# Expert layers of a 512-token block stack: fetch of the first token blocks, split of the first expert's weights and the late rows' bias placed differently

## The reference, cut to what matters

```python
h = rmsnorm(x, ffn_norm[i]) * (1.0 + sc2) + sh2            # adaptive norm
x = x + g2 * hier_moe(h, ...)                              # i = 0, 1

def hier_moe(h, ...):
    g_logits = t @ w_grp + b_grp                           # 4 groups
    g_top, g_idx = top_k(softmax(g_logits), 1)             # one group for a token
    e_logits = (t @ w_rt + b_rt) as (T, 4, 4)
    e_top, e_idx = top_k(e_logits of the group, 2)         # two of its 4 experts
    w = softmax(e_top) * g_top
    hidden = silu(t @ w_gate) * (t @ w_up) * combine       # 16 experts, 1024 -> 256
    return hidden @ w_down                                 # 256 -> 1024
```

## Time and profile before

| | us |
|---|---|
| three timed runs | 3829.78, 3834.50, 3834.51 (median 3834.5) |
| the profiled execution's own time | 3830.91 |
| span of its trace | 3828.5 |
| layer 0: norm, router, experts | from 481.8, 509.5, 542.9 |
| layer 1: norm, router, experts | from 1184.2, 1210.8, 1244.4 |

### The profile page before, as it was taken

One profiled execution on the slowest core, in us unless ns is written; L12 is line 12 of the kernel. 1 busy time (PEld: TensorE's weight loads), 2 busy tenths in 40 slices (PEclk: granted clock), 3 DMA queues, 4 the chain that ended last, 5 costly groups with the idle time before them and its releaser, 6 DMA issues. The chain is left out here.

```text
span 3828.5 us, 45287 instructions
## 1 busy us (share of the span) xinstructions
PE 3060.7 (80%) x15491; PEld 2457.1 (64%) x15491; DVE 2435.3 (64%) x4029; ACT 1271.8 (33%) x2122; POOL 821.3 (21%) x607
## 2 busy tenths in 40 slices
PE   5989849967886899494378464877788999999995
PEld 2876736647665666241256353777788888888884
DVE  1767646545675564566733556887763777877777
ACT  2335334434552543012101012254443333333331
POOL 0001110310120012000012001365453433433331
PEclk9999979988997999696689686898889999999998
DMA  4851359943034896521000012215556888888884
GB/s 181 306 212 31 115 194 359 358 168 118 1 113 158 332 355 252 188 76 36 14 14 1 6 61 67 66 64 164 156 174 237 311 314 333 321 325 327 323 323 176
DMA packets 229526, 701.46 MB, mean 183 GB/s; under 512 B 30054, under 2 KB 109030, under 8 KB 210806
## 3 DMA queue, kind: packets, MB, share of 16 engines
q1 hardware_dynamic: 182428, 478.19, 34.6%
q0 software_dynamic: 46944, 221.27, 15.9%
HBM read 642.20 MB, written 57.18 MB: 183 GB/s over the span
## 5 line engine op out<-in xcount | busy, mean ns | idle before, releaser
L441 PE MATMUL peer_chunks_low<-peer_chunks_down_hi,peer_chunks_bent_hi 128*128 128x512 f32 x768 | 300.1, 391 | 3.6 <-DVE peer_chunks_bent_lo L2751 3.3
L443 PE MATMUL peer_chunks_low<-peer_chunks_down_hi,peer_chunks_bent_lo 128*128 128x512 f32 x768 | 301.0, 392 | 0.0
L442 PE MATMUL peer_chunks_low<-peer_chunks_down_lo,peer_chunks_bent_hi 128*128 128x512 f32 x768 | 300.8, 392 | 0.0
L1350 DVE TENSOR_TENSOR moe_blocks_gu_lo<-moe_raw,moe_blocks_gu_hi 128x2048 fp32r<-128x2048 f32 x112 | 251.6, 2287 | 76.5 <-ACT moe_blocks_gu_hi L1314 76.5
L2625 POOL DMA_INDIRECT peer_chunks_got_up<-in_peer_u_rows,peer_rows_at x128 | 199.9, 1562 | 283.6 <-DVE peer_chunks_got_up L2755 272.7
L441 PE MATMUL peer_chunks_risen<-peer_h_hi,peer_chunks_up_hi 128*128 128x384 f32 x640 | 216.2, 338 | 5.5 <-DVE peer_chunks_up_lo L2732 5.4
L443 PE MATMUL peer_chunks_risen<-peer_h_hi,peer_chunks_up_lo 128*128 128x384 f32 x640 | 215.6, 337 | 0.0
L442 PE MATMUL peer_chunks_risen<-peer_h_lo,peer_chunks_up_hi 128*128 128x384 f32 x640 | 215.1, 336 | 0.0
L1314 ACT CAST moe_blocks_gu_hi<-moe_raw 128x2048 fp32r<-128x2048 f32 x112 | 207.6, 1906 | 15.9 <-DMA moe_raw<-in_moe_gate_up 7.3
L441 PE MATMUL moe_blocks_risen<-moe_blocks_gu_hi,moe_blocks_h_hi 128*128 128x512 f32 x448 | 198.5, 443 | 12.8 <-DVE moe_blocks_gu_lo L1350 8.0
L2631 POOL DMA_INDIRECT peer_chunks_got_down<-in_peer_v,peer_rows_at x128 | 131.3, 1026 | 270.7 <-DVE mod L2767 264.3
(11 more groups left out here) (658 smaller groups left out, 8097.9 us busy)
## 6 DMA issues: line engine op xcount, KB each, us to landing
moe_raw<-in_moe_gate_up SPq DMA_DIRECT2D x32, 2048.0 KB, 9.6
hT<-in_peer_u SPq DMA_DIRECT2D x128, 512.0 KB, 6.9
hT<-in_peer_v SPq DMA_DIRECT2D x128, 512.0 KB, 5.3
fox_o<-in_side_w SPq DMA_DIRECT2D x72, 512.0 KB, 5.9
peer_w<-peer_ahead_stage SPq DMA_DIRECT2D x24, 1024.0 KB, 6.7
peer_chunks_weights<-peer_w SPq DMA_DIRECT2D x128, 192.0 KB, 5.2
moe_raw_dn<-in_moe_down SPq DMA_DIRECT2D x16, 1024.0 KB, 8.9
hT<-in_moe_down SPq DMA_DIRECT2D x16, 1024.0 KB, 7.2
```

The lines of the kernel that those rows point to most:

```text
L441: nc.tensor.matmul(out, l_hi, r_hi, start=start, stop=False)
L442: nc.tensor.matmul(out, l_hi, r_lo, start=False, stop=False)
L443: return nc.tensor.matmul(out, l_lo, r_hi, start=False, stop=stop)
L1350: v.tensor_tensor(gu_lo[:, n % 2, quarter(q)], raw[:, n % GU_SLOTS, quarter(q)], gu_hi[:, n % 2, quarter(q)].bitcast(F32), ALU.subtract).t ...
```

## The change: what it does

- The norm's SP list loads the router's three constants, before the experts' weights, and no longer waits for the stores of `h`; the tiles (`moe_normed`) now live through the router too. The semaphore `rows_out` of the stores goes along to the router.
- The router's POOL list issues the gathers of the first two blocks, after a wait for `rows_out` and for `moe_token`.
- The router's ACT list rounds expert 0's weights before it copies late rows, and its DVE list subtracts at its end (`moe_first_hi`, `moe_first_lo`, which then serve as slot 0 of the pair `gu_hi`, `gu_lo`).
- The experts' stage begins without these, SP's load of step 2 waits for no split, and the first product waits for no split.
- `LateRows`, wherever it stands: POOL's three additions are gone. PE adds the bias by a second matmul of one row into the same bank.

```diff
 class LateRows
     def gpsimd(self, pool):
         self.nc.gpsimd.memset(self.ones[:], 1.0).then_inc(self.filled, 1)
-        pool.wait_ge(self.bias_in, 16)
-        for j in self.ORDER:
-            pool.wait_ge(self.sums_in[j], 16)
-            self.nc.gpsimd.tensor_tensor(self.sums[0:1, j], self.sums[0:1, j], self.bias[:, j], ALU.add).then_inc(self.biased, 1)
     def sum(self, pe, steps):
             pe.wait_ge(self.filled, 1)
-            pe.wait_ge(self.biased, n // self.halves + 1)
+            pe.wait_ge(self.bias_in, 16)
+            pe.wait_ge(self.sums_in[j], 16)
-            self.nc.tensor.matmul(self.banks[n % 2], self.ones[:], self.sums[:, j, columns], start=True, stop=True).then_inc(self.late_summed, 1)
+            self.nc.tensor.matmul(self.banks[n % 2], self.ones[:], self.sums[:, j, columns], start=True, stop=False)
+            self.nc.tensor.matmul(self.banks[n % 2], self.ones[0:1], self.bias[:, j, columns], start=False, stop=True).then_inc(self.late_summed, 1)
 def normed
                         sp.dma_start(rows_dram[t * P:(t + 1) * P], h[:, t]).then_inc(rows_out, 16)
-                    sp.wait_ge(rows_out, 16 * TILES)
 def route
             def _(sp):
-                sp.dma_start(b[:], b_dram).then_inc(loaded, 16)
-                sp.dma_start(earlier[:], earlier_dram).then_inc(loaded, 16)
-                sp.dma_start(number[:], number_dram).then_inc(loaded, 16)
                 late.sync(sp, -1)
             def _(pool):
                 late.gpsimd(pool)
+                pool.wait_ge(rows_out, 16 * TILES)
+                pool.wait_ge(kept, 1)
+                for b in range(2):
+                    pool.indirect_dma_start(rows[:, b], None, rows_dram,
+                                            bass.IndirectOffsetOnAxis(ap=at.token[:, b:b + 1], axis=0)).then_inc(g.rows_in[b], 16)
             def _(act):
                 nc.scalar.activation(ratio[:], gap[:], ACT.Exp).then_inc(raised_ready, 1)
+                act.wait_ge(w_in[0], 16)
+                for part in halves:
+                    nc.scalar.copy(gu_hi[:, part], raw[:, 0, part]).then_inc(gu_rounded, 1)
                 late.keep(act, range(6))
             def _(dve):
                 v.tensor_copy(at.weight[:], table[:, :, 1:]).then_inc(kept, 1)
+                for n, part in enumerate(halves):
+                    dve.wait_ge(gu_rounded, n + 1)
+                    v.tensor_tensor(gu_lo[:, part], raw[:, 0, part], gu_hi[:, part].bitcast(F32), ALU.subtract).then_inc(gu_split, 1)
 def expert_blocks
                 def load_gu(n):
-                    if n >= GU_SLOTS:
-                        sp.wait_ge(gu_split, QUARTERS * (n - GU_SLOTS + 1))
+                    if n > GU_SLOTS:
+                        sp.wait_ge(gu_split, QUARTERS * (n - GU_SLOTS))
-                fetch_rows(0)
-                fetch_rows(1)
-                round_gu(0)
                 round_rows(0)
                 round_gu(1)
-                split_gu(0)
                 split_rows_of(0)
                 split_gu(1)
 def moe
         def early_loads(sp):
+            for dst, src in ((given.b, a["moe_b_route"][layer]), (given.earlier, a["earlier"]), (given.number, a["number"])):
+                sp.dma_start(dst[:], src).then_inc(given.loaded, 16)
             for n in range(GU_SLOTS):
                 sp.dma_start(raw[:, n], gate_up[n]).then_inc(w_in[n], 16)
```

More of the change, by code:

```diff
@@ L315, in scalar, with normed @@
             self.keep(act, range(3 * self.halves))
-def normed(nc, g, name, kind, gain=None, first=None, rows_dram=None, early_loads=None, route_w=None, logits=None):
+def normed(nc, g, name, kind, gain=None, first=None, rows=None, rows_dram=None, rows_out=None, early_loads=None, route_w=None, logits=None):
     SHIFT, SCALE = 0, 1
     with Stage(nc, name) as s:
-        SLOTS = 2 if rows_dram is None else TILES
-        h = s.sb("h", [P, SLOTS, D])
+        SLOTS = 2 if rows is None else TILES
+        h = s.sb("h", [P, SLOTS, D]) if rows is None else rows
         square = s.sb("square", [P, D])
@@ L932, in _, with route @@
                 divide(LOOPS - 1, LOOP - 1)
-def route(nc, g, name, logits, b_dram, earlier_dram, number_dram, at, late):
+def route(nc, g, name, logits, given, early, at, rows, rows_dram, rows_out, raw, gu_hi, gu_lo, w_in, late):
     N, MORE = GROUPS + EXPERTS, TOKEN_BLOCKS - GROUPS
     with Stage(nc, name) as s:
-        b = s.sb("b", [P, N])
-        earlier, number = s.sb("earlier", [P, P]), s.sb("number", [P, TILES])
+        s.adopt([given.loaded, rows_out], early)
+        b, earlier, number, loaded = given.b, given.earlier, given.number, given.loaded
         earlier_ones = s.sb("earlier_ones", [P, 2, P], BF16)
@@ L976, in route @@
         iota = lambda n: g.iota[:, :n].unsqueeze(1).to_broadcast([P, TILES, n])
+        halves = [slice(j * KD // 2, (j + 1) * KD // 2) for j in range(2)]
         with s.block() as block:
@@ L1125, with expert_blocks @@
 GU_SLOTS, DN_SLOTS = 2, 4
-def expert_blocks(nc, g, name, layer, at, raw, raw_dn, w_in, dn_in, early, rows_dram, out_dram, gate_up, down, gate_row):
+def expert_blocks(nc, g, name, layer, at, raw, raw_dn, rows, first, w_in, dn_in, early, rows_dram, out_dram, gate_up, down, gate_row):
     STEPS, BLOCKS_, HALVES, FK = TOKEN_BLOCKS * PER_GROUP, TOKEN_BLOCKS, D // BANK, D_EXPERT // P
@@ L2964, in moe @@
         raw_dn = own.enter_context(nc.sbuf_tensor(f"{name}_raw_dn", [P, 2, D_EXPERT // P, D], F32))
-        early = ExitStack()
+        rows = own.enter_context(nc.sbuf_tensor(f"{name}_fetched_rows", [P, 2, D], F32))
+        first = [own.enter_context(nc.sbuf_tensor(f"{name}_first_{x}", [P, KD, BANK], F32R)) for x in ("hi", "lo")]
+        early, early_route = ExitStack(), ExitStack()
         w_in = [early.enter_context(nc.semaphore(f"{name}_w_in{u}")) for u in range(GU_SLOTS)]
@@ L2972, in moe @@
         at.row = own.enter_context(nc.sbuf_tensor(f"{name}_row", [P, TOKEN_BLOCKS - GROUPS, PER_GROUP], U32))
+        given = Global()
+        given.loaded, rows_out = (early_route.enter_context(nc.semaphore(f"{name}_{x}")) for x in ("given", "rows_out"))
+        given.b = own.enter_context(nc.sbuf_tensor(f"{name}_b", [P, GROUPS + EXPERTS], F32))
+        given.earlier = own.enter_context(nc.sbuf_tensor(f"{name}_earlier", [P, P], F32))
+        given.number = own.enter_context(nc.sbuf_tensor(f"{name}_number", [P, TILES], F32))
         def early_loads(sp):
+            for dst, src in ((given.b, a["moe_b_route"][layer]), (given.earlier, a["earlier"]), (given.number, a["number"])):
+                sp.dma_start(dst[:], src).then_inc(given.loaded, 16)
             for n in range(GU_SLOTS):
```

33 lines of the change are left out of this document (17 added, 16 removed).

## The result

Slower. The changed kernel took 3859.87 us (median of 4 runs, 3857.17 to 3861.06) against 3832.14 for the kernel before (4 runs): a ratio of 1.0074 (95% interval 1.0056 to 1.0091), +27.7 us. The forecast was 3805. The profiled execution took 3857.17, with a span of 3855.4.

A forecast was written before the change was run, and what follows sets the result against it. PE, busy 80% of the span, was taken as the bound. Terms -3.4 - 4.1 - 9.6 + 9.6 - 18.4 - 1.1 = -27.0 us took the profiled 3830.9 to 3803.9; it said 3805, range 3796 to 3819.

The forecast's parts named there:

- 2 and 3, constants and stretched instructions: Router: constants land during the norm, -4.1 us; DVE instructions no longer stretched beside POOL's additions, -9.6 us.
- part 4: Bias matmuls in the routers: six more in each layer at 0.85 us each, all on the path, +9.6 us.
- part 6: Three output projections: PE adds the bias without waiting for POOL; -3.6, +1.2 and +1.3, together -1.1 us.
- Rival A: Late rows: one-row matmuls don't hold the clock up, twelve take 20.4 us; +12.5 us, 3843.4 in all; chance 0.04.
- part 1: Norm's end: without the wait for the stores of `h` only a barrier of 0.6 is left, -3.4 us.
- Part 3: Router's DVE chain: instructions stretched during POOL's additions return to 0.17 us each, -9.6 us.
- rival C: Router: the stretched DVE instructions have another cause than POOL and stay, 3815 us; chance 0.03.
- Part 5: Experts' start: SP's load no longer waits for the gathers, step 2 lands 9.2 us sooner per layer, -18.4 us.
- rival B: Experts' start: step 2's load is no sooner relative to the work, 3809 to 3818 us; chance 0.07.
- Rival D: Router's end: the gathers are late; if landing took 5 us more, 10 of 18.4 would go, 3815; chance 0.04.

The follow-up runs named there:

- e5: The kernel before, unchanged, profiled once more: 3823.56 us.
- e4: The changed kernel with both matmuls of each late pair reading one row (sums of partitions 1 to 127 left out): 3843.82 us, ratio 1.0039.
- f1: The changed kernel with both late matmuls over 64 rows, bias and partitions 64 to 127 left out: 3846.57 us in one execution.
- e8: The changed kernel with each second late matmul reading 64 rows of the sums, no bias: 3862.55 us in one execution.
- e7: The changed kernel with both banks' sums first, then both one-row bias matmuls, same work: 3815.54 us in one execution.
- e1: The changed kernel without the six bias matmuls, the bias left out of the result: 3777.95 us, ratio 0.9864.
- e6: The kernel before with only the bias part: one-row matmuls instead of POOL's additions: 3881.73 us, ratio 1.0134.
- e2: The changed kernel with the bias added by POOL as before, all other parts kept: 3806.5 us, ratio 0.9939.
- e3: The changed kernel with each bias matmul reading 128 rows, 127 of them zero, same result: 3810.03 us, ratio 0.9948.

## Why the prediction was wrong

From the two profiles, stage by stage, with the forecast in the last column:

| step | layer 0 / 1, or the three projections | sum | forecast |
|---|---|---|---|
| 1, norm's end | -2.4, -2.6 | -4.9 | -3.4 |
| 2 and 3, constants and stretched instructions | -7.3, -6.2 | -13.5 | -13.7 |
| 4, bias matmuls in the routers (`table` to the last copy) | +16.9, +15.6 | +32.6 | +9.6 |
| 5, experts' start (last copy to the stage's end) | -8.9, -8.5 | -17.3 | -18.4 |
| 6, output projections' start | +9.8, +11.9, +10.7 | +32.4 | -1.1 |
| the projections themselves, starting at a low clock | +1.4 to +2.0 each | +5 | 0 |

Together +35, against 26.9 between the two spans. The difference lies in stages that the change doesn't touch, above all `peer`, 11.3 us shorter in the second profile (e5 shows how far it varies).

**The step that failed** is "so each costs 0.85" in part 4, and with it part 6. The number of matmuls, their place on the path and what waits behind them were right; the price was not. I took it from the six sums at full clock and from one-row matmuls of `ada` (587 to 692 ns a record), assuming that the clock would rise under the new mix as it did under full matmuls. It is 2.00: 1.70 at the half clock, which never rises (1.70 in e4 and f1 too), and 0.30 for each change of height (e8 against f1: 2.00 and 1.70). In `ada` one matmul in nine reads one row and eight full ones in a row stand around it, so that row could not price a stretch in which every second one does. e7, with the same twelve matmuls in another order, shows how much the neighbours decide. Nor was 0.85 right for `ada` itself: in the kernel before, at full clock, the next matmul starts 1.05 us after the one-row matmul does, so the change of height was in the trace.

```profile
27.71 1.12 PE L170 MATMUL ada_acc<-ada_bias,ada_ones 1*128 x2
28.76 7.13 PE L169 MATMUL ada_acc<-ada_ring,ada_c_rep 128*128 128x512 f32 x16
```

Part 6 also counted on the full clock in `fox_out`; it fell at 423.3, 0.2 us after the late rows began there.

Rival A named this mechanism, put it at 3843.4 and gave it 0.04. It had 1.70 for a matmul and so missed the 0.30 (60 matmuls in five places, 18 us); with it A gives 3861, the result. e4, twelve matmuls of 1.70 without a change of height, came out 13.6 above the kernel before; A had 12.5. The chance was too small: no row of the trace spoke for the clock rising in such a mix, and none against. The Trainium skill ("TensorE: Matmul & The Clock Gate", What's actually happening), on which I leaned, releases the clock by how busy PE is. Here PE was busy 8.00 of 8 us and the clock stayed at 0.50, so that rule as I read it doesn't hold here, nor for matmuls of 64 rows alone (f1).

Point by point otherwise: the barrier of part 1 takes 0.4 and not 0.6. The rest of what part 1 gave beyond the forecast is luck: in layer 1 PE's own part of the norm took 23.8 us against 25.1 before, and over all the runs it varies from 23.8 to 25.9. Part 3's cause is shown (rival C falls): the changed kernel, e1 and e6 have no POOL addition in the router and no stretched instruction of that chain; e2 has the additions, and the stretches of 1.2 to 2.2 us are back. Part 5 is right to the half microsecond: PE's third product starts 20.0 us after the last copy (584.49 - 564.52), forecast 19.6, with a stall of 1.8, forecast 1.3; rival B falls.

Rival D costs nothing in the changed kernel, where 24 us of late rows cover the gathers, but it is real: in e1 and e2 the router ends with the gathers, 11.8 and 11.9 us after `table` starts, and the experts start 2.2 and 2.6 us after the last copy instead of 0.3. The forecast's late rows of 12 us would have covered them, as e3's 13.3 did (0.3).

## What to carry to other kernels

A matmul's price goes with the granted clock that its own surroundings earn, so before adding matmuls that read few rows (bias rows, for one) to a stretch that starts at half clock, find a row in which such matmuls stand as densely as they would in the new code; if there is none, the half-clock price is a case with a real chance. Where such matmuls are needed, padding them to full height brought the time from 3859.9 to 3810.0 here (e3), and grouping them behind full ones to 3815.5 in a single execution (e7), with one place of five still at half clock. Neither is free: without bias matmuls it was 3778. Better still, add a bias where an engine already passes over the accumulator, off the path.

## What the runs showed that I had not expected

- Matmuls that read 64 rows, back to back for 20 us, stayed at 0.50; of 96 rows, or of 128 rows and 64 columns, they reached 1.00 between 2.4 and 6.2 us after the first of them. Whether the border lies at 65 or at 96 rows wasn't tried.
- A change of height between neighbouring matmuls cost 0.30 us at half clock (2.00 against 1.70).
- A single full matmul between lower ones never raised the clock (the changed kernel, e8); with two in a row it was up in four places of five (e7). What decides isn't settled.
- DVE instructions of 0.17 us took 1.2 to 2.2 us beside POOL's additions on one partition (e2), one for each addition, and none did where the additions were gone (e1, e6).
- POOL's issue of a gather took 0.94, 2.39 or 6.86 us with what DVE ran beside it. That DVE's work is the cause fits the three traces and wasn't tested by itself.
